# The first attention's weighted sum of values with the values stationary: four heads' probabilities moving, two groups as column tiles, a transposed result

## The reference, cut to what matters

```python
k_cmp = partial_rope(compress(k_cmp_in, w_cmp_k), cmp_start)   # 15 compressed blocks
v_cmp = compress(v_cmp_in, w_cmp_v)
# for each of the three kinds: softmax(q k^T / 8, masked) * gate, times the values of the head's group
mixed = gate_nsa * (o_nsa @ w_br_nsa) + gate_hg * (o_hg @ w_br_hg)   # o_nsa: 256 x 512
x = x + mixed @ w_out
x = x + hier_moe(rmsnorm(x, ffn_norm), ...)
```

## Time and profile before

| | us |
|---|---|
| three timed runs, median (lowest to highest) | 1981.9 (1976.75 to 1983.2) |
| the profiled execution, device time | 1984.58 |
| its span in the trace | 1982.8 |
| first block up to its router (0 to about 324) | 324 |
| first mixture (343 to 812), DMA share 0.98 | 469 |
| second block's attention and state space part (812 to 1030) | 218 |
| second mixture (1030 to 1943), DMA share 1.00 | 913 |

### The profile page before, as it was taken

One profiled execution on the slowest core, in us unless ns is written; L12 is line 12 of the kernel. 1 busy time (PEld: TensorE's weight loads), 2 busy tenths in 40 slices (PEclk: granted clock), 3 DMA queues, 4 the chain that ended last, 5 costly groups with the idle time before them and its releaser, 6 DMA issues. The chain is left out here.

```text
span 1982.8 us, 21454 instructions
## 1 busy us (share of the span) xinstructions
PE 1614.6 (81%) x8740; PEld 744.9 (38%) x8740; DVE 486.8 (25%) x773; ACT 238.2 (12%) x413; POOL 108.6 (5%) x262
## 2 busy tenths in 40 slices
PE   6999987666666756388869889898898998888996
PEld 6666645222122222175443333333333333333332
DVE  2622313101011101479442121122112122112123
ACT  2224311100000000014110000000000000000000
POOL 0020000890000000000000000000000000000000
PEclk9999997878788787699869999999999999999998
DMA  9556653999999999622239999999999999999994
GB/s 330 194 205 214 256 204 128 406 421 421 421 421 421 421 421 421 229 96 97 99 150 429 427 427 428 428 428 428 427 428 427 420 428 428 427 427 428 427 428 188
DMA packets 100868, 686.74 MB, mean 346 GB/s; under 512 B 17959, under 2 KB 19160, under 8 KB 51416
## 3 DMA queue, kind: packets, MB, share of 16 engines
q1 hardware_dynamic: 96066, 679.12, 83.5%
q10 hardware_dynamic: 4758, 7.01, 1.1%
HBM read 685.06 MB, written 1.05 MB: 346 GB/s over the span
## 5 line engine op out<-in xcount | busy, mean ns | idle before, releaser
L1295 PE MATMUL ps<-ring,hT 128*64 128x512 f32 x2048 | 449.9, 597 | 29.4 <-DMA ring<-in_w_dram 29.3
L1322 PE MATMUL ps<-ring,m_hidT 128*64 128x512 f32 (+1 forms) x1536 | 313.5, 666 | 56.7 <-DMA ring<-in_w_down_dram 31.8
L1295 PEld LDWEIGHTS ps<-ring,hT 128*64 128x64 f32 x2048 | 153.6, 138 | 323.7 <-issue 323.7
L1291 PE MATMUL ps<-ring,hT 128*32 128x512 f32 x1024 | 161.5, 789 | 110.0 <-DMA ring<-in_w_up_dram 67.6
L1322 PEld LDWEIGHTS ps<-ring,m_hidT 128*64 128x64 f32 (+1 forms) x1536 | 95.3, 140 | 258.2 <-issue 235.6
L1397 DVE TENSOR_SCALAR Wp<-ps 128x1024 f32<-128x1024 f32 x16 | 19.6, 1225 | 453.7 <-PE ps L1295 453.7
L1291 PEld LDWEIGHTS ps<-ring,hT 128*32 128x32 f32 x1024 | 41.6, 139 | 228.3 <-issue 181.3
L872 PE MATMUL ps<-ring,hT 128*128 128x512 f32 (+1 forms) x288 | 120.8, 573 | 0.0
L1334 PE MATMUL ps<-hT,m_GT 128*128 128x512 f32 x192 | 88.6, 604 | 29.5 <-DVE hT L1413 22.3
L1348 ACT ACTIVATE m_sg<-Wp 128x1024 f32<-128x1024 f32 x16 | 16.9, 1057 | 794.1 <-DVE Wp L1397 794.1
L1248 PEld LDWEIGHTS ps<-m_Pm,hn 128*128 128x128 f32 x832 | 99.4, 199 | 21.9 <-issue 21.2
(11 more groups left out here) (412 smaller groups left out, 1278.5 us busy)
## 6 DMA issues: line engine op xcount, KB each, us to landing
ring<-in_w_dram SPq DMA_DIRECT2D x192, 2048.0 KB, 15.8
ring<-in_w_gate_dram SPq DMA_DIRECT2D x32, 2048.0 KB, 19.3
ring<-in_w_up_dram SPq DMA_DIRECT2D x32, 2048.0 KB, 20.9
ring<-in_w_down_dram SPq DMA_DIRECT2D x32, 2048.0 KB, 20.4
ring<-in_w_in_dram SPq DMA_DIRECT2D x14, 2048.0 KB, 15.7
ring<-in_w_ada_dram SPq DMA_DIRECT2D x12, 2048.0 KB, 11.4
ring<-in_w_out_dram SPq DMA_DIRECT2D x4, 2048.0 KB, 9.0
ring<-in_w_br_hg_dram SPq DMA_DIRECT2D x1, 2048.0 KB, 7.9
```

Of the source, the lines that this page charges most:

```text
L1291: ins = nt.matmul(ps[r, u // 2, :], xgT[:, 4 * HALVES[u] + t, r], w[:, c:c + 512], start=u % 2 == 0 and t == 0, stop=u % 2 == 1 and t == 3 ...
L1295: ins = nt.matmul(ps[64 * e:64 * e + 64, b, :], xgT[:, 2 * u + t, 64 * e:64 * e + 64], w[:, c:c + 512], start=False, stop=u == 3 and t == ...
L1322: ins = nt.matmul(ps[r, C0 + h, :], hidT[:, n * u + t, r], w[:, c:c + 512], start=u == 0 and t == 0, stop=n * u + t == FT - 1, tile_positi ...
```

## The change

- `Qv(n)`: for every key tile and group one matmul with the 64 value columns of the group stationary and the transposed probabilities of its four heads, 512 columns, moving. Group g writes partitions 64g to 64g + 63 of the output bank, as a column tile at (0, 64g). 12 matmuls in the program for the four steps in place of 48.
- The output bank now holds (group, width) on the partitions and (s, r, token) in the columns, that is, it is already transposed. The compressed attention is one matmul with the block-diagonal `vcb` stationary and all of `PcT[:, i]`, 512 columns, moving, in place of four.
- ScalarE copies the bank directly into `onT`; `Nout`, its transposes, its two copies and its two semaphores are gone.
- `Bn` reads chunk c of `onT` and the matching chunk 2(c % 2) + c // 2 of the branch weights. So that the rows match, `w_br_nsa` is loaded by two DMAs of 64 partitions each, one for each group; the first signals a new semaphore. `Bn` waits for both, for the last copy of `PT`, and for the tile's copy of the output just ahead of the tile's matmuls.

```diff
--- before.py
+++ after.py
@@ -122,6 +122,7 @@
         ident = K("ident")
         ring_ready = [S(f"ring_ready{j}") for j in range(RING)]
         units_used = S("units_used")
+        s_brn = S("nsa_branch_rows_in")
 
 
         units = []
@@ -139,7 +140,7 @@
 
         ORDER = "A0 F0 F1 Hpre F2 F3 H0 F4 H1 F5 H2 F6 H3 F7 H4 F8 H5 F9 H6 Nrope F10 H7 F11 H8 A1 Nqk F12 Ho Nkv F13 Gate Hgate " \
                 "Ncmp A2 Ht F14 Nkc F15 Nsc A3 F16 Npc A4 M0 F17 Qt0 A5 Qv0 SigH M1 F18 Qt1 A6 Qv1 M2 F19 A7 A8 Qt2 A9 Qv2 M3 F20 F21 " \
-                "Bh0 Qt3 A10 SigN Qv3 Bh1 A11 Nout Bn"
+                "Bh0 Qt3 A10 SigN Qv3 Bh1 A11 Bn"
         FILL = [w for w in ORDER.split() if w[0] in "FA" and w[1].isdigit()]
         PLACE = {}
         for w in ORDER.split():
@@ -209,6 +210,12 @@
                 if k >= RING:
                     sp.wait_ge(ring_ready[k % RING], 16 * (k // RING))
                 sp.sem_inc(ring_ready[k % RING], 16)
+                return
+            if k == K_BR_NSA:
+                for g in range(2):
+                    sp.dma_start(ring[64 * g:64 * g + 64, k % RING, :].rearrange("p (r n) -> p r n", r=4),
+                                 A["w_br_nsa"][0].rearrange("(g r d) n -> g d r n", g=2, r=4)[g]).then_inc(
+                        (s_brn, ring_ready[k % RING])[g], 16)
                 return
             if K_MOE1 <= k < K_IN2:
                 src, dst = moe1_src(0, k - K_MOE1), moe1_dst(k)
@@ -394,8 +401,7 @@
         Wc = mf[:, 2048:4096].rearrange("p (l e) -> p l e", l=32)
         P = hnf.rearrange("p (s a k) -> p s a k", s=2, a=4)
         PT = W1[:, 1024:3072].rearrange("p (b h q) -> p b h q", b=2, h=8)
-        onsa = junk[:].rearrange("p (i c) -> p i c", i=2)
-        onT = grow[:].rearrange("p (a q) -> p a q", a=4)
+        onT = grow[:].rearrange("p (i r q) -> p i r q", i=2, r=4)
 
         hq, hf = hqT[:].rearrange("p h t -> p (h t)"), hfT[:].rearrange("p h t -> p (h t)")
         Dl = hf
@@ -425,7 +431,7 @@
             "cmp_scores", "cmp_shifted", "cmp_exp", "cmp_probs", "cmp_probsT", "cmp_probsT_kept"))
         s_s, s_mx, s_exp, s_p, s_pt, s_ptk, s_pv = (S(n) for n in (
             "scores", "scores_max", "scores_exp", "probs", "probsT", "probsT_kept", "pv_done"))
-        s_o, s_oT, s_oTk = S("nsa_out_kept"), S("nsa_outT"), S("nsa_outT_kept")
+        s_o = S("nsa_out_kept")
         h_f, h_ln, h_d, h_e, h_qk, h_a, h_am = (S(n) for n in (
             "forget", "log_forget", "level_exponents", "level_factors", "level_operands", "level_products", "level_added"))
         h_o, h_sq, h_v, h_r, h_n, h_g, h_t, h_tk, h_lb = (S(n) for n in (
@@ -804,14 +810,9 @@
                     i, ty = STEPS[n]
                     if ty:
                         a.wait_ge(s_pv, n + 1)
-                        na.activation(onsa[:, i], ps[:, i, :], ACT.Copy).then_inc(s_o, 1)
+                        na.activation(onT[:, i].rearrange("p r q -> p (r q)"), ps[:, i, :], ACT.Copy).then_inc(s_o, 1)
                     if n == 3:
                         a.dma_start(X[:], A["x"][0].rearrange("(i q) d -> q i d", i=NT)).then_inc(s_x, 16)
-
-                def Nout():
-                    a.wait_ge(s_oT, 1)
-                    for b in range(2):
-                        na.activation(onT[:, 2 * b:2 * b + 2], ps[:, 2 + b, :].rearrange("p (a q) -> p a q", a=2), ACT.Copy).then_inc(s_oTk, 1)
 
                 def Bn():
                     a.wait_ge(b_m, 2)
@@ -827,7 +828,7 @@
                     n1.act_tiles(a, N1_BANKS)
 
                 follow(dict(F=F, A=Ada, Hpre=Hpre, H=H, Ho=Ho, Gate=Gate, SigH=SigH, SigN=SigN, Nqk=Nqk, Nkv=Nkv, Nkc=Nkc, Nsc=Nsc,
-                            Npc=Npc, Ht=Ht, M=M, Qt=Qt, Qv=Qv, Nout=Nout, Bn=Bn))
+                            Npc=Npc, Ht=Ht, M=M, Qt=Qt, Qv=Qv, Bn=Bn))
 
             @block.tensor
             def _(pe):
@@ -984,10 +985,7 @@
                     ins.then_inc(s_s, 1)
                     if ty == 0:
                         pe.wait_ge(h_tk, 2)
-                        for r in range(4):
-                            o = ps[:, i, :].rearrange("p (g r d) -> p g r d", g=2, r=4)[:, :, r, :]
-                            nt.matmul(o, PcT[:, i, r, :], vcb.rearrange("p (g d) -> p g d", g=2), start=r == 0, stop=False,
-                                      skip_group_check=True)
+                        nt.matmul(ps[:, i, :], vcb, PcT[:, i].rearrange("p (r s) q -> p s r q", s=2), start=True, stop=False, skip_group_check=True)
 
                 def Qt(n):
                     i, ty = STEPS[n]
@@ -1001,12 +999,12 @@
                 def Qv(n):
                     i, ty = STEPS[n]
                     pe.wait_ge(s_ptk, [1, 2, 4, 6][n])
-                    for s8 in range(8):
-                        h = 2 * (s8 % 4) + s8 // 4
-                        for kb in range(i + 1):
-                            c = 896 + 256 * ty + (h // 4) * 64
-                            ins = nt.matmul(ps[:, i, h * 64:h * 64 + 64], PT[:, kb, s8, :], qkv[:, kb, c:c + 64],
-                                            start=False, stop=(ty == 1 and s8 == 7 and kb == i), skip_group_check=True)
+                    for kb in range(i + 1):
+                        for g in range(2):
+                            c = 896 + 256 * ty + g * 64
+                            ins = nt.matmul(ps[64 * g:64 * g + 64, i, :], qkv[:, kb, c:c + 64],
+                                            PT[:, kb].rearrange("p (s g r) q -> p s g (r q)", s=2, g=2)[:, :, g],
+                                            start=False, stop=ty == 1 and kb == i, tile_position=(0, 64 * g), skip_group_check=True)
                     ins.then_inc(s_pv, 1)
 
                 def Bh(i):
@@ -1024,26 +1022,19 @@
                         pe.wait_ge(units_used, K_BR_HG)
                         pe.sem_inc(units_used, FREES["Bh1"])
 
-                def Nout():
-                    pe.wait_ge(s_o, 2)
-                    pe.wait_ge(s_ptk, 6)
-                    for i in range(NT):
-                        for c in range(4):
-                            ins = nt.transpose(ps[:, 2 + c // 2, (c % 2) * 256 + i * 128:(c % 2) * 256 + i * 128 + 128],
-                                               onsa[:, i, c * 128:c * 128 + 128], ident)
-                    ins.then_inc(s_oT, 1)
-
                 def Bn():
                     unit_arrived(pe, K_BR_NSA)
-                    pe.wait_ge(s_oTk, 2)
+                    pe.wait_ge(s_brn, 16)
+                    pe.wait_ge(s_ptk, 6)
                     pe.wait_ge(s_pev, len(FILL))
                     for i in range(NT):
+                        pe.wait_ge(s_o, i + 1)
                         if i:
                             pe.wait_ge(b_hm, 2)
                         for h in range(2):
                             for c in range(4):
-                                ins = nt.matmul(ps[:, 4 + 2 * i + h, :], onT[:, c, i * 128:i * 128 + 128],
-                                                unit(K_BR_NSA)[:, c, h * 512:h * 512 + 512], start=c == 0, stop=c == 3)
+                                ins = nt.matmul(ps[:, 4 + 2 * i + h, :], onT[:, i, c, :],
+                                                unit(K_BR_NSA)[:, 2 * (c % 2) + c // 2, h * 512:h * 512 + 512], start=c == 0, stop=c == 3)
                         ins.then_inc(b_m, 1)
                     for t in range(KC):
                         for i in range(NT):
@@ -1070,7 +1061,7 @@
                     n1.pe_tiles(pe, N1_BANKS, q1_in, 64, q1_lg, wr1, brow1, 36, N1_LOGITS)
 
                 follow(dict(F=F, A=Ada, H=H, Ho=Ho, Ht=Ht, Nqk=Nqk, Nkv=Nkv, Ncmp=Ncmp, Nkc=Nkc, Nsc=Nsc, Npc=Npc, M=M, Qt=Qt, Qv=Qv,
-                            Bh=Bh, Nout=Nout, Bn=Bn))
+                            Bh=Bh, Bn=Bn))
         p1.close()
 
 
```

## The result

The changed kernel takes 1975.26 us (median of 20 runs, 1971.62 to 1981.29); the kernel before, timed 20 times in all, 1984.12 us (1976.75 to 1988.52). The ratio is 0.9962 with a 95% interval of 0.9953 to 0.9971: 7.5 us less, 5.8 to 9.3. (The two medians alone lie 8.9 us apart; the ratio, which has the interval, is what the text goes by.) A second series on another occasion gave 1975.33 us and 0.9962 again (0.9948 to 0.9976). The forecast was 1974.7 us, from 7.20 us gained on a median of 1981.9.

A forecast was written before the change was run, and what follows sets the result against it. Computing on TensorE ahead of the first mixture, not loading, was taken as the bound; Qv 5.39 + Nout 1.81 = 7.20 us off the median 1981.9 gave 1974.7 us, range 1969.5 to 1980.0 us (8 in 10).

The forecast's parts named there:

- The first mixture's start decides: Before the first mixture, computing and not loading sets the time; savings ahead of 343 us come out whole at the end.
- Qv, 5.39 us: Main term: Qv's four steps shrink to 1.01, 1.01, 1.88 and 1.88 us, saving 0.90 + 0.92 + 1.83 + 1.74 us.
- the bounds: Total gain if Qv's layout changes cost 0 or 0.3 us a step instead of 0.15: 7.8 or 6.6 us.
- The limit by the table load: ScalarE's table load before step 1's exponentials ends at 186.62 us, so only 0.90 us of step 0's saving counts.
- The compressed attention, 0: In M(0) and M(2), 0.98 us becomes 0.86; the 0.12 us gained twice is lost waiting for VectorE, counted 0.
- Nout, 1.81 us: Ahead of Bn: without Nout's transposes and copies, Bn waits only for A11's copy and starts 1.81 us earlier.
- Split load, 0: Loading the branch weights in two halves costs nothing, with 23 us of cover before Bn wants them.
- The rule from the Trainium skill: Weight loads overlap running matmuls only when the row group differs; by it Qv's two tiles would take turns.
- the first rival: Qv's two column tiles do not overlap: gain 2.1 us in all, 1979.8 us; chance 0.12.
- Rival 2: Each Qv step's first instruction runs alone, 0.43 us a step, 1.7 in all: gain 5.5 us, 1976.4 us; chance 0.12.
- Rival 3, the clock: TensorE's clock stays up before the first mixture in most new runs: 5 us more gained, 1969.7 us; chance 0.05.
- Rival 4, late halves: The split branch weights land too late for Bn, over 43.7 us from issue; 1988 us and more at 57; chance 0.03.

The follow-up runs named there:

- e1: Changed kernel with Qv's column tiles taken away, each matmul taking 128 stationary value columns; ratio to the kernel before 0.9994.
- e2: Changed kernel with Nout's eight transposes and two ScalarE copies put back as ballast that Bn waits for; ratio to the kernel before 0.9975.
- e3: Kernel before with only the branch weights' load split into two DMAs of 64 partitions, the projection waiting for both; ratio 1.0011.
- e11: Kernel before with only the branch weights' load split into two DMAs, the same kernel run again in another series; ratio 0.9996.
- e5: Changed kernel with A11 placed ahead of Bh1 in the hand-written order; ratio to the kernel before 0.9940.
- e4: Changed kernel with Qv's two loops exchanged, all key tiles of group 0 before those of group 1; ratio to the kernel before 0.9965.
- e7: Changed kernel with useless filler matmuls, four and nine, in two TensorE waits ahead of the first mixture; ratio to the kernel before 0.9932, median 1971.08 us.
- e8: Changed kernel with A11 ahead of Bh1, tile 0's transposes first in Bn, and filler matmuls together; ratio to the kernel before 0.9925, median 1970.49 us.
- e9: Changed kernel with A11 ahead of Bh1 and filler matmuls, eight in the second wait, without reordered transposes; ratio to the kernel before 0.9943.

## Why the prediction was right, point by point

- **The first mixture's start decides, and what is saved before it arrives whole.** Shown. Qv and Nout gave 6.93 to 7.06 us at Bn, 7.05 to 7.33 at the mixture, 7.5 (5.8 to 9.3) in the times. e1 and e2 take away 5.1 and 1.7 us at Bn and lose 0.0032 and 0.0013 in the ratio, 6.3 and 2.6 us, within their intervals. The mixture's first matmul stood at 335.75, forecast near 336, and Bn at 255.78, forecast near 256.0 and just behind A11's copy.
- **Qv, 5.39 us.** Measured 5.38 (e2). Each step was forecast at 1.01 and 1.88 us, and took 1.01 and 1.86 to 1.87. What carried it was taking the price from the second mixture's rows, of the same shape. In the bounds, no cost for the layout changes would have given 7.65 us in all and not 7.8, since step 0 was already held at 0.90 by the table load.
- **The limit by the table load, 0.90 instead of 0.92.** The trace after has the exponential 0.02 us behind the end of the load. A Qv(0) shorter still would bring nothing at step 1.
- **The compressed attention, 0.** It takes 197.84 - 196.89 = 0.95 us, not 0.86, against 0.98; a change of layout stands behind it here too. For step 2 the reason given holds, the wait of 0.24 us for VectorE. For step 0 it does not: the prediction has a similar wait there, but both traces show the transposes following at once, without one. The 0.12 us would have counted once; as the instructions were 0.03 us shorter and not 0.12, it made no difference.
- **Nout, 1.81 us.** Mis-sized by 0.15: 1.66. Bn began 0.25 us after the end of A11's copy (255.78 - 255.53), where I had taken the 0.10 us that stood behind the copy by line 814. e3 and e11 show the same 0.25 us in the kernel before, where only the split load and its one wait ahead of the wait for the copies were put in; in e2, with the wait for the copies ahead of the new ones, it is 0.11. So the 0.15 us goes with the waits at Bn and not with which copy is last. Which of them makes it was not tried.
- **Split load, 0.** Shown by e3 and e11 together.
- **The rule from the Trainium skill** ("TensorE: Matmul & The Clock Gate", Part 3) says that weight loads overlap running matmuls only for another row group. That the tiles would then take turns, the first rival, is the prediction's own step from loads to matmuls. This case's runs go against it: both tiles take all rows and overlap fully (1.87 us for eight, 3.5 to 3.6 without tiles). Rival 2, a start paid in each step, falls by the same rows.
- **Rival 3, the clock.** The stretch did run at the low clock in both profiles of the changed kernel; it takes work in the wait to change that. In none of the ten traces without filler did it stay up through the norm and the logits (16 logit matmuls in 3.46 or 3.47 us each time), so the 5 us carried downward for such an execution stand for something that no run shows. Executions of one kernel spread over 10 us; I had put the spread down to this stretch. The table speaks against it as the main cause: Bn to mixture varies from 79.7 to 81.9 us in the kernels without filler, the part behind the mixture's start by 7 us.
- **Rival 4, late halves.** Excluded. In the changed kernel the halves are issued at 210.4 and 216.2 and land 21.8 to 22.5 us later, the second so at least 17 us ahead of Bn. The prediction's 23 us left out that the second issue comes 6 us behind the first.
- **The base.** The median of three runs before, 1981.9, lay 2.2 us under that of twenty. On 1984.12 the same sum gives 1976.9, 1.7 us above what was measured. So the closeness of 1974.7 to 1975.3 is partly luck; the gain by the ratio, 7.2 against 7.5 with an interval of 3.5 us, is not told apart.

## What to carry to other kernels

Swapping stationary and moving operand pays only for what it lets overlap or leaves out: here 96 short matmuls behind 128-column weight loads and 24 long ones in series cost nearly the same (11.2 and 11.0 us), and nearly the whole gain of the step came from two tiles of 64 columns running at once; look for a row of the same shape elsewhere in the trace and price it by that. A layout that comes out already transposed saves its transposes and also a round trip through another engine. Put work between two stages so that the copy that frees its bank is over when the next stage wants the bank: A11 ahead of the other branch's projection brought Bn 1.28 us forward. Then follow the gain to the stage that counts, for in that trace it was gone before the mixture (e5).

## What the runs showed of the hardware

- Two tiles of 64 columns over all rows overlap even when four instructions of one stand in the program ahead of four of the other: 1.87 us for eight of 0.43 us (e4). The price of a matmul with 512 moving columns is 0.43 us with 64 or 128 stationary columns alike.
- In some executions the transposes ahead of the output projection ran at 1.2 GHz behind their wait of 2.46 us for VectorE (15 of them in 3.46 us in e7, in 1.86 in the changed kernel), and in others not, with the same order of work up to there: e3 and e11 are one kernel and have 1.86 and 3.35. It costs about 1.5 us when it happens. In e11, then the clock in e7:

```profile
279.94 3.35 PE L1059 MATMUL ps<-CS,mrg 128*128 128x128 f32 x15 [2.47 <-DVE mrg L678]
```

```profile
272.70:276.00 3.30, 3.27 (x16) 3.27 (x17) 0.00 (x0) 1.79 (x3) 0.00 (x0) 0.50 1.11 241
```

- Four matmuls of 512 columns in the wait of 4.0 us ahead of the logits kept the granted clock at 1.00 through the first 16 logit matmuls in all three kernels that had them (1.87 us in e7, e8 and e9, 3.47 without). In each of the three it fell once further on, at the end of the logits (e7, e9) or at the gather (e8).
